# Modulation items of 1024 columns instead of 512 in a transformer kernel on one core

## The chip, the cores and the metric

The kernel runs on one core of a Trainium2 chip. The core has five engines with instruction queues of their own: TensorE (PE, with weight loads shown as PEld), VectorE (DVE), ScalarE (ACT), GpSimd (POOL) and SyncE (SP). Engines wait for each other by semaphores, and 16 DMA engines move data between HBM and the on-chip SBUF. The metric is the time of one execution in microseconds (us), measured on the device. All data are float32.

## The reference, cut to what matters

Eight sublayers work in turn on a sequence x of 256 tokens and 1024 features. In the first four (a hybrid mixer, a feed-forward layer, a dilated attention, a feed-forward layer) the normalized input is scaled and shifted, and the output gated, by vectors made from one conditioning vector c:

```python
def modulation(c, w, b):
    return jnp.split(jax.nn.silu(c) @ w + b, 3, axis=-1)

def sandwich(x, mod, g_pre, g_post, fn):
    shift, scale, gate = mod
    h = rms_norm(x, g_pre) * (1.0 + scale[:, None]) + shift[:, None]
    return x + gate[:, None] * rms_norm(fn(h), g_post)
...
        x = sandwich(x, modulation(c, ada_w[layer, 0], ada_b[layer, 0]), norm_pre[layer, 0], norm_post[layer, 0], mixer)
        x = sandwich(x, modulation(c, ada_w[layer, 1], ada_b[layer, 1]), norm_pre[layer, 1], norm_post[layer, 1], ffn)
```

So there are four modulations j = 0 to 3, each a vector of 1024 times a matrix `ada_w[j // 2, j % 2]` of 1024 rows and 3072 columns. Its columns are three parts of 1024: shift, scale and gate. Each matrix has 12 MB, and every element is used once.

## The kernel before

Every engine has one program, written out by hand; the order in the code is the order on the engine.

**Weights of the layers.** SP loads them in pieces of 1 MB into the six slots of `raw`. ScalarE casts a half of a piece (128 x 1024) to `whi` (L542), and VectorE subtracts it from the raw value to get the remainder `wlo` (L1299, called a split). TensorE multiplies with both. `whi` and `wlo` hold four halves. A raw slot is loaded again when VectorE has split both halves.

**Modulation.** The product of c with a matrix is not made on TensorE directly. VectorE multiplies 128 rows of a matrix with the matching 128 values of silu(c), which stand as a column `sc[:, k:k+1]`, and adds them to an accumulator (`acc_a` or `acc_b`, 128 partitions). After eight such items (k = 0 to 7) TensorE sums over the partitions with a matrix of ones (`sum_cols`, `sum_gates`). The first block of columns that TensorE needs (shift and scale of j = 0) comes through `raw` (`ada_first`) and isn't touched here. Everything later goes through `ada_ring`, which GpSimd fills: two halves, each of 4 row groups of 128 rows and 512 columns (1 MB). A half `kh` is loaded again when its four items are done:

```python
                        if b:
                            pool.wait_ge(s["ada_step"], 8 * (b - 1) + 4 * (kh + 1))
                        src, _ = src_cols(t["ada_w"][j // 2, j % 2], n, kh)
```

A block b has 512 columns and eight items, and there are 20 blocks (gate of j = 0, all of j = 1, 2, 3). VectorE works on them in `ada_item`, at places between its other work:

- In the hybrid mixer's input projection (`hyb_in`), two blocks and a half stand after groups of four splits. Then come the eight HGRN levels, `for i in range(8)`: `level(i)` (L1747 to L1749) multiplies decays, `merge(i - 1)` (L1731) picks scores, then a split, then one item (three at i = 6 and i = 7). TensorE's `level_scores(i)` waits for level and merge of the rounds before. L1719 is the product that opens the levels, L1764 the subtraction that gives the first half of `hlo` for the output projection.
- In the output projection, blocks 4 and 5; the last two items (k = 6, 7) of the last 512 scale columns are done by TensorE out of the ring (`PE_LAST`).
- In the first feed-forward layer, half a block at a time, after two splits.
- In the qkv projections, four splits (`proj`) and then a whole block of eight items, six times.

In the qkv stage TensorE needs four halves for a block of 512 output features: per half two groups of rows, four feature tiles and three products, 96 matmuls in all (`proj_half`, `three`).

Of the kernel before, what the change touches and what calls it, by code (L numbers as in the profile page):

```python
# [18 lines left out]
F32 = mybir.dt.float32  # L19
F32R = mybir.dt.float32r  # L20
ALU = mybir.AluOpType
# [67 lines left out]
def program(nc, t):  # L89

    with ExitStack() as ctx:
# [27 lines left out]
        with ExitStack() as first:  # L119
            ada_ring = sb(first, "ada_ring", [P, 2, 4, 512])  # L120
# [215 lines left out]
        DVE_LAST, PE_LAST = (4, 5), (6, 7)  # L336
# [117 lines left out]
        def _(pool):  # L454
            def ada_blocks(first, blocks):

                for i, (j, n) in enumerate(blocks):
                    b = first + i
                    for kh in range(2):
                        if b:  # L460
                            pool.wait_ge(s["ada_step"], 8 * (b - 1) + 4 * (kh + 1))
                        src, _ = src_cols(t["ada_w"][j // 2, j % 2], n, kh)
                        pool.dma_start(ada_ring[:, kh, :, :], src).then_inc(ada_in[kh], 16)  # L463
# [21 lines left out]
            SHIFT_SCALE, GATE = [0, 512, 1024, 1536], [2048, 2560]  # L485
            pool.wait_ge(s["ada_used"], ADA_FIRST)
            ada_blocks(0, [(0, n) for n in GATE])
            gain_row(0)
            ada_blocks(2, [(1, n) for n in SHIFT_SCALE])
            ada_blocks(6, [(1, GATE[0])])  # L490
            gain_row(1)
            ada_blocks(7, [(1, GATE[1])] + [(2, n) for n in SHIFT_SCALE + GATE])
# [5 lines left out]
            ada_blocks(14, [(3, SHIFT_SCALE[0])])  # L498
            gain_row(3)
            ada_blocks(15, [(3, n) for n in SHIFT_SCALE[1:] + GATE])  # L500
# [782 lines left out]
        def _(dve):  # L1283
# [18 lines left out]
            def ada_item(acc, b, n, k, it=0, bias=None):  # L1302

                kh, kk = k // 4, k % 4
                if kk == 0:
                    dve.wait_ge(ada_in[kh], 16 * (b + 1) + 32 * it)
                out = acc[:, bass.ds(n, 512)]
                if k == 0 and bias is not None:
                    dve.wait_ge(s[f"wrow_in{bias}"], 16)
                    ins = V.scalar_tensor_tensor(out=out, in0=ada_ring[:, kh, kk, :], scalar=sc[:, k:k + 1],  # L1310
                                                 in1=gg[:, bias, n:n + 512], op0=ALU.mult, op1=ALU.add)
                elif k == 0:
                    ins = V.tensor_scalar(out, ada_ring[:, kh, kk, :], sc[:, k:k + 1], None, ALU.mult)
                else:
                    dve.wait_ge(s["ada_step"], 8 * b + k + 16 * it)
# [4 lines left out]
            def ada_part(acc, b, n, kh, it=0, bias=None):  # L1320

                for kk in range(4):
                    ada_item(acc, b, n, 4 * kh + kk, it, bias)
# [1868 lines left out]
```

## Time and profile before

| what | value |
|---|---|
| median of 3 runs | 1269.61 us (1267.96 to 1271.66) |
| the profiled execution, its own time | 1269.97 us |
| its span, from the first to the last instruction | 1268.2 us |
| mean granted TensorE clock | 0.995 of full |
| TensorE busy | 1248.5 us (98%) |
| VectorE busy | 933.9 us (74%) |
| ScalarE busy | 718.2 us (57%) |
| moved by DMA | 274.41 MB, 216 GB/s over the span |

The profile is of one execution. Busy time is the time in which an engine has an instruction at work; the ends of matmuls are modelled, so a busy TensorE may hold short idle times. A share of the span is an average over stages whose limits differ.

### The profile page before, as it was taken

The numbers are of one execution on the slowest core, as the hardware profiler recorded it, in microseconds if no ns is written. First come the engines' busy times: TensorE is split into PE (matmuls) and PEld (weight loads), VectorE is DVE, ScalarE is ACT, GpSimd is POOL, SyncE is SP. The second block draws the span as 40 slices with busy tenths as digits, with TensorE's granted clock in tenths as the row PEclk, the third lists the DMA queues.
The fourth block names the chain that finished last, engine by engine and source line by source line (L and its number), as shares of the span: only waits on it lengthen the run. The fifth ranks groups of instructions, "written<-read, shape, count | busy, mean of one in ns | idle before, by whom it ended". The sixth has DMA issues, their size and how long they took to land.

```text
span 1268.2 us, 20841 instructions
## 1 busy us (share of the span) xinstructions
PE 1248.5 (98%) x8024; PEld 1133.6 (89%) x8024; DVE 933.9 (74%) x1222; ACT 718.2 (57%) x1069; POOL 50.8 (4%) x76
## 2 busy tenths in 40 slices
PE   8999999999999999999999999999999999999999
PEld 6998899999999778999989989888888888888888
DVE  6889988886899658666676695676666677666665
ACT  3676754444744557444467764665555667655554
POOL 1101000000111000000001000000000000000000
PEclk8999999999999999999999999999999999999999
DMA  9986989996799734666556544356565542366650
GB/s 348 372 297 208 339 290 325 334 327 205 244 361 370 230 67 153 206 203 200 199 166 211 162 150 155 132 198 200 200 202 202 190 163 95 122 220 204 202 166 34
DMA packets 147248, 274.41 MB, mean 216 GB/s; under 512 B 4759, under 2 KB 85679, under 8 KB 147048
## 3 DMA queue, kind: packets, MB, share of 16 engines
q1 hardware_dynamic: 132320, 220.21, 51.5%
q0 software_dynamic: 13616, 50.94, 11.9%
q10 hardware_dynamic: 1240, 2.26, 0.5%
q8 instruction: 49, 0.80, 0.3%
q14 instruction: 23, 0.19, 0.0%
HBM read 272.30 MB, written 1.10 MB: 216 GB/s over the span
## 4 chain that ended last, share of the span: by engine, by line
PE 82%; DVE 8%; DMA 4%; ACT 3%; issue 2%; ACTq 0%; POOL 0%; DVEq 0%; POOLq 0%
PE ps L2229 80%; DMA ada_ring<-in_ada_w 4%; DVE wlo L1299 2%; DVE acc_a L1316 2%; ACT whi L542 1%; PE ps L2682 1%; DMA voh<-in_voh 1%; ACT xn L603 0%; PE ps L2416 0%; PE ps L2399 0%; DVE rs L1949 0%; ACT h L659 0%; DVE prob L1906 0%; ACT hboth L654 0%; PE ps L2976 0%
## 5 line engine op out<-in xcount | busy, mean ns | idle before, releaser
L1299 DVE TENSOR_TENSOR wlo<-raw,whi 128x1024 fp32r<-128x1024 f32 x400 | 483.5, 1222 | 222.8 <-ACT whi L542 222.0
L542 ACT CAST whi<-raw 128x1024 fp32r<-128x1024 f32 x400 | 416.6, 1048 | 404.0 <-PE ps L2229 389.6
L2229 PE MATMUL ps<-hboth,whi 128*128 128x256 f32 (+1 forms) x2720 | 605.2, 311 | 1.0 <-DVE hboth L1529 0.5
L2229 PE MATMUL ps<-hboth,wlo 128*128 128x256 f32 x1792 | 491.6, 274 | 0.7 <-DVE hboth L1524 0.4
L2229 PEld LDWEIGHTS ps<-hboth,whi 128*128 128x128 f32 x2720 | 447.2, 191 | 30.1 <-issue 6.2
L2229 PEld LDWEIGHTS ps<-hboth,wlo 128*128 128x128 f32 x1792 | 343.9, 192 | 3.1 <-issue 0.6
L2229 PE MATMUL ps<-whi,hidhi 128*128 128x512 f32 x434 | 164.5, 379 | 0.0
L2229 PE MATMUL ps<-wlo,hidhi 128*128 128x512 f32 x434 | 164.1, 378 | 0.0
L2229 PE MATMUL ps<-whi,hidlo 128*128 128x512 f32 x434 | 164.1, 378 | 0.0
L2229 PE MATMUL ps<-whi,hboth 128*128 128x512 f32 (+1 forms) x512 | 155.8, 375 | 3.0 <-DVE wlo L1299 0.9
L2229 PEld LDWEIGHTS ps<-whi,hboth 128*128 128x128 f32 x512 | 95.5, 190 | 18.5 <-issue 5.1
L1316 DVE SCALAR_TENSOR_TENSOR acc_a<-ada_ring,sc,acc_a 128x512 f32<-128x512 f32 (+1 forms) x124 | 93.1, 751 | 7.6 <-DMA ada_ring<-in_ada_w 3.7
L2229 PE MATMUL ps<-wlo,hboth 128*128 128x512 f32 (+1 forms) x256 | 93.8, 366 | 0.0
L2229 PEld LDWEIGHTS ps<-whi,hidlo 128*128 128x128 f32 x434 | 82.0, 189 | 11.5
L2229 PEld LDWEIGHTS ps<-wlo,hidhi 128*128 128x128 f32 x434 | 82.1, 189 | 11.4 <-issue 0.2
L2229 PEld LDWEIGHTS ps<-whi,hidhi 128*128 128x128 f32 x434 | 82.2, 189 | 10.5 <-ACT whi L542 0.2
L2229 PEld LDWEIGHTS ps<-wlo,hboth 128*128 128x128 f32 x256 | 48.7, 190 | 6.2 <-issue 1.0
L463 POOL DMA_DIRECT2D ada_ring<-in_ada_w x40 | 30.0, 751 | 296.0 <-DVE acc_a L1316 212.6
L1651 DVE TENSOR_REDUCE tmp<-ps 128x512 f32<-128x1024 f32 x32 | 38.9, 1217 | 3.5 <-PE ps L2229 3.5
L1656 DVE TENSOR_TENSOR hidlo<-hid,hidhi 128x512 fp32r<-128x512 f32 x32 | 22.1, 692 | 16.6 <-ACT hidhi L760 16.6
L603 ACT ACTIVATE xn<-x 128x512 f32<-128x512 f32 (+1 forms) x32 | 19.3, 602 | 10.7 <-DVE x L1418 5.7
L755 ACT ACTIVATE tmp<-tmp 128x512 f32<-128x512 f32 x32 | 20.1, 627 | 2.9 <-DVE tmp L1651 2.9
(259 smaller groups left out, 1118.6 us busy)
## 6 DMA issues: line engine op xcount, KB each, us to landing
raw<-in_ffn_w_in SPq DMA_DIRECT2D x44, 1024.0 KB, 7.2
ada_ring<-in_ada_w POOLq DMA_DIRECT2D x40, 1024.0 KB, 7.9
raw<-in_w_mlp_up SPq DMA_DIRECT2D x32, 1024.0 KB, 5.4
raw<-in_w_mlp_down SPq DMA_DIRECT2D x32, 1024.0 KB, 4.9
raw<-in_ffn_w_out SPq DMA_DIRECT2D x22, 1024.0 KB, 5.1
raw<-in_att_w_qkv SPq DMA_DIRECT2D x18, 1024.0 KB, 7.3
raw<-in_w_in_even SPq DMA_DIRECT2D x18, 1024.0 KB, 5.1
raw<-in_hyb_w_in SPq DMA_DIRECT2D x10, 1024.0 KB, 11.2
```

The lines of the kernel that those rows point to most:

```text
L463: pool.dma_start(ada_ring[:, kh, :, :], src).then_inc(ada_in[kh], 16)
L542: A.copy(whi[:, H % 4, :], raw[:, slot(n), h * HALF:(h + 1) * HALF]).then_inc(s["hi_ready"], 1)
L603: A.activation(xn_of(j)[0][:, i // 2, c], x[:, i // 2, c], ACT.Square, accum_out=stat[:, 4 + i:5 + i]).then_inc(s["ssq_x"], 1)
L755: A.activation(tmp2[:, g % 3, :], tmp2[:, g % 3, :], ACT.Relu).then_inc(s["mrelu"], 1)
L1299: V.tensor_tensor(wlo[:, H % 4, :], raw[:, slot(n), h * HALF:(h + 1) * HALF], whi[:, H % 4, :].bitcast(F32), ALU.subtract).then_inc(s["lo_ ...
L1316: ins = V.scalar_tensor_tensor(out=out, in0=ada_ring[:, kh, kk, :], scalar=sc[:, k:k + 1], in1=out, op0=ALU.mult, op1=ALU.add)
L1651: V.tensor_reduce(in_order(tmp2[:, g % 3, :], 2), parts_of(UP_BANK[g % 3]), AX, ALU.add) \
L1656: V.tensor_tensor(hidlo2[:, g % 3, :], hid2[:, g % 3, :], hidhi2[:, g % 3, :].bitcast(F32), ALU.subtract).then_inc(s["mhid_lo"], 1)
L2229: return pe.matmul(out, lhsT, rhs, start=first, stop=last, skip_group_check=True)
L2682: m = pe.transpose(dl_turned(p, i)[:, (j - j0) * P:(j - j0 + 1) * P], dl_block(p, j), ident[:, :])
```

## The change

The blocks of 512 columns become whole parts of 1024 columns, w = 0 to 9. A load takes 256 rows (2 groups of 128) of a whole part instead of 512 rows of half a part. It still has 1 MB, but rows of 4 KB. The ring keeps its size: two slots of 1 MB, now `[P, 2, 2, D]`, and a slot is loaded again after two items. There are as many loads, 40, and half as many items. Where VectorE did eight items of a block it now does four items of 1024 columns. In the qkv stage they stand one by one between the splits. TensorE's share is now one item (k = 7) of all 1024 scale columns instead of two of 512.

```diff
-            ada_ring = sb(first, "ada_ring", [P, 2, 4, 512])
+            ada_ring = sb(first, "ada_ring", [P, 2, 2, D])
...
-        DVE_LAST, PE_LAST = (4, 5), (6, 7)
+        PE_LAST = 7
...
+            def ada_loads(first, rows):
+
+                for i, (j, n, q) in enumerate(rows):
+                    l = first + i
+                    if l >= 2:
+                        pool.wait_ge(s["ada_step"], 2 * (l - 1))
+                    src, _ = src_down(t["ada_w"][j // 2, j % 2][:, n:n + D], 2 * P * q)
+                    pool.dma_start(ada_ring[:, l % 2, :, :], src).then_inc(ada_in[l % 2], 16)
...
+            def ada_item(acc, w, n, k, it=0, bias=None):
+
+                q, kk = k // 2, k % 2
                 if kk == 0:
-                    dve.wait_ge(ada_in[kh], 16 * (b + 1) + 32 * it)
-                out = acc[:, bass.ds(n, 512)]
+                    dve.wait_ge(ada_in[q % 2], 16 * (2 * w + q // 2 + 1) + 32 * it)
+                out, row = acc[:, bass.ds(n, D)], ada_ring[:, q % 2, kk, :]
...
                     if ada:
-                        ada_part(*ada, 0, it, bias)
+                        ada_items(*ada, (4 * (g % 2), 4 * (g % 2) + 1), it, bias)
                     split_some(g, it, after[:2])
                     if ada:
-                        ada_part(*ada, 1, it)
+                        ada_items(*ada, (4 * (g % 2) + 2, 4 * (g % 2) + 3), it)
                     split_some(g, it, after[2:])
...
             proj("hyb_in", HYB[0:1], 0)
-            ada_block(acc_a, 0, 0, 0)
+            ada_items(acc_a, 0, 0, range(4), 0, 0)
             proj("hyb_in", HYB[1:2], 1)
-            ada_block(acc_a, 1, 512, 0)
+            ada_items(acc_a, 0, 0, range(4, 8))
             for q in range(4):
                 split(2 * (FIRST["hyb_in"] + 4) + 4 + q)
                 if q == 1:
-                    ada_part(acc_a, 2, 512 * 2, 0)
+                    ada_items(acc_a, 1, D, range(2))
...
-                for q in range(i, i + 1) if i < 6 else range(3 * i - 12, 3 * i - 9):
-                    b, k = (q + 20) // 8, (q + 20) % 8
-                    ada_item(acc_a, b, 512 * b, k)
-                    if q == 9:
-                        dve.wait_ge(s["hyb_hi"], 1)
-                        V.tensor_tensor(hlo[:, 0:4, :], y1[:, 0:4, :], hhi[:, 0:4, :].bitcast(F32), ALU.subtract) \
-                            .then_inc(s["hyb_lo"], 1)
-            ada_part(acc_a, 4, 512 * 4, 0)
+                if 1 <= i <= 6:
+                    ada_item(acc_a, 1, D, i + 1)
+                if i == 7:
+                    dve.wait_ge(s["hyb_hi"], 1)
+                    V.tensor_tensor(hlo[:, 0:4, :], y1[:, 0:4, :], hhi[:, 0:4, :].bitcast(F32), ALU.subtract) \
+                        .then_inc(s["hyb_lo"], 1)
+                    ada_item(acc_a, 2, 2 * D, 0)
+            ada_item(acc_a, 2, 2 * D, 1)
             split(2 * FIRST["hyb_in"] + 23)
-            ada_part(acc_a, 4, 512 * 4, 1)
+            ada_items(acc_a, 2, 2 * D, range(2, 4))
...
             for b in range(8):
-                proj("qkv", (QKV_B * 2 + QKV_A)[b:b + 1], b)
-                if b < 6:
-                    ada_block(acc_a, 14 + b, 512 * b)
+                for q in range(4):
+                    split(2 * (FIRST["qkv"] + 2 * b) + 4 + q)
+                    if b < 6:
+                        ada_item(acc_a, 7 + b // 2, D * (b // 2), 4 * (b % 2) + q)
...
             for i in range(16):
                 m = mm(ps[:, 0, i:i + P], acc_a[:, 1024 + i * P:1024 + (i + 1) * P], ones[:, :])
-                for k in PE_LAST if i >= 12 else ():
-                    m = mm(ps[:, 0, i:i + P], ada_ring[:, 1, k - 4, (i - 12) * P:(i - 11) * P],
-                           sc[:, k:k + 1].to_broadcast([P, P]), False, True)
-            m.then_inc(s["ada_step"], len(PE_LAST))
+                if i >= 8:
+                    m = mm(ps[:, 0, i:i + P], ada_ring[:, 1, 1, (i - 8) * P:(i - 7) * P],
+                           sc[:, PE_LAST:PE_LAST + 1].to_broadcast([P, P]), False, True)
+            m.then_inc(s["ada_step"], 1)
```

The instructions of VectorE in order, first where the last two HGRN levels stand. `acc_a` items are the modulation's, `wlo` is a split, `att` a merge, and `hboth<-y,hboth` the first `hlo` subtraction. Before:

```order
L1316 SCALAR_TENSOR_TENSOR acc_a<-ada_ring,sc,acc_a 128x512 [waits ada_step]
L1747 TENSOR_TENSOR bandqk<-pooled,tot 128x16x32 [waits hg_step,hg_copied,hg_scores]
L1748 TENSOR_TENSOR bandqk<-sq,tot 128x16x32
L1749 TENSOR_TENSOR f<-tot 128x16
L1299 TENSOR_TENSOR wlo<-raw,whi 128x1024 [waits hi_ready]
L1316 SCALAR_TENSOR_TENSOR acc_a<-ada_ring,sc,acc_a 128x512 [waits ada_step] x2
L1316 SCALAR_TENSOR_TENSOR acc_a<-ada_ring,sc,acc_a 128x512 [waits ada_step,ada_in1]
L1747 TENSOR_TENSOR pooled<-bandqk,f 128x8x64 [waits hg_step,hg_copied,hg_scores]
L1748 TENSOR_TENSOR sq<-bandqk,f 128x8x64
L1749 TENSOR_TENSOR tot<-f 128x8
L1316 SCALAR_TENSOR_TENSOR acc_a<-ada_ring,sc,acc_a 128x512 [waits ada_step]
L1764 TENSOR_TENSOR hboth<-y,hboth 128x1024 [waits hyb_hi]
```

and now (all lines of the kernel's VectorE part have moved by 1 or 5):

```order
L1321 SCALAR_TENSOR_TENSOR acc_a<-ada_ring,sc,acc_a 128x1024 [waits ada_step,ada_in1]
L1748 TENSOR_TENSOR bandqk<-pooled,tot 128x16x32 [waits hg_step,hg_copied,hg_scores]
L1749 TENSOR_TENSOR bandqk<-sq,tot 128x16x32
L1750 TENSOR_TENSOR f<-tot 128x16
L1304 TENSOR_TENSOR wlo<-raw,whi 128x1024 [waits hi_ready]
L1321 SCALAR_TENSOR_TENSOR acc_a<-ada_ring,sc,acc_a 128x1024 [waits ada_step]
L1748 TENSOR_TENSOR pooled<-bandqk,f 128x8x64 [waits hg_step,hg_copied,hg_scores]
L1749 TENSOR_TENSOR sq<-bandqk,f 128x8x64
L1750 TENSOR_TENSOR tot<-f 128x8
L1764 TENSOR_TENSOR hboth<-y,hboth 128x1024 [waits hyb_hi]
L1318 TENSOR_SCALAR acc_a<-ada_ring,sc 128x1024 [waits ada_in0]
L1321 SCALAR_TENSOR_TENSOR acc_a<-ada_ring,sc,acc_a 128x1024 [waits ada_step]
```

In level 6's round and after it, three items and one of 512 columns stood before level 7 and the `hlo` subtraction; now it is one of 1024, and the next part's first item follows the subtraction.

The second place is VectorE in the qkv stage, the sixth block of splits and items. Before:

```order
L1299 TENSOR_TENSOR wlo<-raw,whi 128x1024 [waits hi_ready] x4
L1313 TENSOR_SCALAR acc_a<-ada_ring,sc 128x512 [waits ada_in0]
L1316 SCALAR_TENSOR_TENSOR acc_a<-ada_ring,sc,acc_a 128x512 [waits ada_step] x3
L1316 SCALAR_TENSOR_TENSOR acc_a<-ada_ring,sc,acc_a 128x512 [waits ada_step,ada_in1]
L1316 SCALAR_TENSOR_TENSOR acc_a<-ada_ring,sc,acc_a 128x512 [waits ada_step] x3
```

and now:

```order
L1304 TENSOR_TENSOR wlo<-raw,whi 128x1024 [waits hi_ready]
L1321 SCALAR_TENSOR_TENSOR acc_a<-ada_ring,sc,acc_a 128x1024 [waits ada_step,ada_in0]
L1304 TENSOR_TENSOR wlo<-raw,whi 128x1024 [waits hi_ready]
L1321 SCALAR_TENSOR_TENSOR acc_a<-ada_ring,sc,acc_a 128x1024 [waits ada_step]
L1304 TENSOR_TENSOR wlo<-raw,whi 128x1024 [waits hi_ready]
L1321 SCALAR_TENSOR_TENSOR acc_a<-ada_ring,sc,acc_a 128x1024 [waits ada_step,ada_in1]
L1304 TENSOR_TENSOR wlo<-raw,whi 128x1024 [waits hi_ready]
L1321 SCALAR_TENSOR_TENSOR acc_a<-ada_ring,sc,acc_a 128x1024 [waits ada_step]
```

The four splits in a row and the eight items after them have become four pairs of a split and an item, and the waits for the two halves of the ring (`ada_in0`, `ada_in1`) now stand two splits apart. A tensor_scalar, which opens a part of columns, stands in every block before and in every second one now.

## Rows read from the trace of the kernel before

**Rows 1.** The page: busy time by engine, and the last chain's shares by engine.

```profile
PE 1248.5 (98%) x8024; PEld 1133.6 (89%) x8024; DVE 933.9 (74%) x1222; ACT 718.2 (57%) x1069; POOL 50.8 (4%) x76
...
PE 82%; DVE 8%; DMA 4%; ACT 3%; issue 2%; ACTq 0%; POOL 0%; DVEq 0%; POOLq 0%
```

**Rows 2.** Windows: us; busy us of PE, PEld, DVE, ACT, POOL; PEclk, DMA share, GB/s.

```profile
79.00:93.00 14.00, 13.15 (x82) 11.47 (x81) 14.00 (x17) 7.99 (x14) 0.75 (x1) 1.00 0.69 237
...
113.00:130.00 17.00, 15.65 (x83) 13.33 (x84) 14.99 (x21) 10.79 (x15) 2.25 (x3) 1.00 0.83 269
...
366.00:377.00 11.00, 11.00 (x101) 11.00 (x100) 10.02 (x13) 5.39 (x6) 1.50 (x2) 1.00 1.03 379
```

**Rows 3.** Timeline of VectorE, 36 to 135 us: start us, us, instruction, [idle before].

```profile
76.29 0.49 DVE L1313 TENSOR_SCALAR acc_a<-ada_ring,sc 128x512 f32<-128x512 f32 x1 [1.54 <-DMA ada_ring<-in_ada_w]
...
81.33 1.22 DVE L1719 TENSOR_TENSOR bandqk<-f 128x1024 f32<-128x1024 f32 x1
...
98.22 0.75 DVE L1316 SCALAR_TENSOR_TENSOR acc_a<-ada_ring,sc,acc_a 128x512 f32<-128x512 f32 x1
98.89 0.69 DVE L1747 TENSOR_TENSOR bandqk<-pooled,tot 128x512 f32<-128x512 f32 x1
...
109.81 2.38 DVE L1316 SCALAR_TENSOR_TENSOR acc_a<-ada_ring,sc,acc_a 128x512 f32<-128x512 f32 x3
112.11 0.69 DVE L1747 TENSOR_TENSOR pooled<-bandqk,f 128x512 f32<-128x512 f32 x1
...
114.05 1.22 DVE L1764 TENSOR_TENSOR hboth<-y,hboth 128x1024 fp32r<-128x1024 f32 x1
...
117.24 0.75 DVE L1313 TENSOR_SCALAR acc_a<-ada_ring,sc 128x512 f32<-128x512 f32 x1 [0.52 <-DMA ada_ring<-in_ada_w]
```

**Rows 4.** Timeline of TensorE at four of the level scores.

```profile
87.91 2.05 PE L2229 MATMUL ps<-pooled,sq 128*128 128x128 f32 x16 [0.60 <-DVE att L1731]
...
97.37 1.95 PE L2229 MATMUL ps<-pooled,sq 128*128 128x128 f32 x16
...
101.84 1.95 PE L2229 MATMUL ps<-bandqk 128*128 128x128 f32 x16
...
113.57 1.13 PE L2229 MATMUL ps<-pooled,sq 128*128 128x128 f32 x8 [0.85 <-issue]
```

**Rows 5.** Timeline of TensorE in the qkv stage, two of its repeating pieces.

```profile
365.07 0.39 PE L2229 MATMUL ps<-hboth,whi 128*128 128x256 f32 x2
...
365.41 0.39 PE L2229 MATMUL ps<-hboth,whi 128*128 128x256 f32 x2
```

**Rows 6.** Timeline of VectorE, qkv stage.

```profile
374.47 3.11 DVE L1316 SCALAR_TENSOR_TENSOR acc_a<-ada_ring,sc,acc_a 128x512 f32<-128x512 f32 x4 [0.56 <-DMA ada_ring<-in_ada_w]
377.50 4.62 DVE L1299 TENSOR_TENSOR wlo<-raw,whi 128x1024 fp32r<-128x1024 f32 x4
...
411.03 4.62 DVE L1299 TENSOR_TENSOR wlo<-raw,whi 128x1024 fp32r<-128x1024 f32 x4
```

**Rows 7.** Waits, 330 to 440 us: total us, times, longest us.

```profile
PE ps L2229 <- DVE wlo L1299: 0.9, 1, 0.9
```

**Rows 8.** Groups by line and shape, 0 to 430 us: count, busy us, mean ns.

```profile
L1316 DVE SCALAR_TENSOR_TENSOR acc_a<-ada_ring,sc,acc_a 128x512 f32<-128x512 f32 x82 | 61.6, 751 | 6.4 <-DMA ada_ring<-in_ada_w 3.7
...
L1455 DVE TENSOR_SCALAR xn<-x,small 128x1024 f32<-128x1024 f32 x2 | 1.5, 745 | 0.0
```

**Rows 9.** The tile ada_ring: count, ns min/median/max; and its transfers.

```profile
L1313 DVE TENSOR_SCALAR acc_a<-ada_ring,sc x16: 477/480/748, 76.3 to 404.3; 128x512 f32<-128x512 f32 x10, 128x512 f32 x6
...
DMA to landing us min/median/max: 5.6/7.9/10.8
```

**Rows 10.** The page's DMA issues: count, KB each, median us to landing.

```profile
raw<-in_w_mlp_up SPq DMA_DIRECT2D x32, 1024.0 KB, 5.4
raw<-in_w_mlp_down SPq DMA_DIRECT2D x32, 1024.0 KB, 4.9
```

**Rows 11.** Timeline of GpSimd: one issue of an ada load.

```profile
117.01 0.75 POOL L463 DMA_DIRECT2D ada_ring<-in_ada_w  x1 [4.63 <-DVE acc_a L1316]
```

More of the change, by code:

```diff
@@ L484, in _, with part_rows @@
             bias_row(1)
-            SHIFT_SCALE, GATE = [0, 512, 1024, 1536], [2048, 2560]
+            def part_rows(j, part):
+                return [(j, part * D, q) for q in range(4)]
+            SHIFT, SCALE, GATE = range(3)
             pool.wait_ge(s["ada_used"], ADA_FIRST)
-            ada_blocks(0, [(0, n) for n in GATE])
+            ada_loads(0, part_rows(0, GATE))
             gain_row(0)
-            ada_blocks(2, [(1, n) for n in SHIFT_SCALE])
-            ada_blocks(6, [(1, GATE[0])])
+            ada_loads(4, part_rows(1, SHIFT) + part_rows(1, SCALE))
+            ada_loads(12, part_rows(1, GATE)[:2])
             gain_row(1)
-            ada_blocks(7, [(1, GATE[1])] + [(2, n) for n in SHIFT_SCALE + GATE])
+            ada_loads(14, part_rows(1, GATE)[2:])
+            ada_loads(16, part_rows(2, SHIFT) + part_rows(2, SCALE) + part_rows(2, GATE))
             gain_row(2)
@@ L1300, in split, with ada_items @@
                                 whi[:, H % 4, :].bitcast(F32), ALU.subtract).then_inc(s["lo_ready"], 1)
[L1302 to L1304 removed]
+            def ada_item(acc, w, n, k, it=0, bias=None):
+                q, kk = k // 2, k % 2
                 if kk == 0:
[L1306 to L1307 removed]
+                    dve.wait_ge(ada_in[q % 2], 16 * (2 * w + q // 2 + 1) + 32 * it)
+                out, row = acc[:, bass.ds(n, D)], ada_ring[:, q % 2, kk, :]
                 if k == 0 and bias is not None:
                     dve.wait_ge(s[f"wrow_in{bias}"], 16)
[L1310 to L1311 removed]
+                    ins = V.scalar_tensor_tensor(out=out, in0=row, scalar=sc[:, k:k + 1], in1=gg[:, bias, :],
+                                                 op0=ALU.mult, op1=ALU.add)
                 elif k == 0:
[L1313 removed]
+                    ins = V.tensor_scalar(out, row, sc[:, k:k + 1], None, ALU.mult)
                 else:
[L1315 to L1317 removed]
+                    dve.wait_ge(s["ada_step"], 8 * w + k + 8 * it)
+                    ins = V.scalar_tensor_tensor(out=out, in0=row, scalar=sc[:, k:k + 1], in1=out, op0=ALU.mult,
+                                                 op1=ALU.add)
                 ins.then_inc(s["ada_step"], 1)
[L1320 to L1323 removed]
+            def ada_items(acc, w, n, ks, it=0, bias=None):
+                for k in ks:
+                    ada_item(acc, w, n, k, it, bias)
             def ada_first(a):
```

39 lines of the change are left out of this document (13 added, 26 removed).

## Prediction

> **What bounds the kernel now.** I read the page first. TensorE is busy for 98% of the span, VectorE for 74%, and the chain that ended last is 82% TensorE, 8% VectorE and 4% DMA [rows 1]. Freed VectorE time is therefore worth something only where TensorE stands still for VectorE. The second view is the table of stretches: see where TensorE's busy time falls short of the window. It does so in 79 to 93 us (13.15 of 14.00, VectorE busy 14.00 of 14.00) and in 113 to 130 us (15.65 of 17.00); in 366 to 377 us it is not short at all (11.00 of 11.00), while the DMA share is 1.03 [rows 2]. So two places matter: the HGRN levels inside the first projection, where VectorE is the packed engine, and the qkv projections, where the transfers are.
>
> In the levels, see two waits of TensorE: before the scores at 87.91 us it stood 0.60 us for VectorE's merge (L1731), and before those at 113.57 us 0.85 us [rows 4]; the latter follow level 7 of VectorE, which starts at 112.11 us because three items of modulation stand before it from 109.81 us [rows 3]. In the qkv stage the whole loss is one wait of 0.9 us for a split [rows 7], that of the burst at 411.03 us [rows 6].
>
> How much is there to win? The shortfalls of the two windows are 0.85 + 1.35 us, with the 0.9 us of the qkv stage 3.1 us. The ends of matmuls are modelled, so some idle time may be hidden; I allow up to 4.5 us. All other stretches with modulation run with TensorE full or wait for something else.
>
> **The change, part by part.**
>
> *The items.* 160 items of 512 columns (158 on VectorE, 2 on TensorE) become 80 of 1024 (79 and 1). A scalar_tensor_tensor of 512 takes 751 ns [rows 8]. No trace row has one of 1024 with both inputs in SBUF, so I take the slope of tensor_tensor: 0.69 us for 512 columns (98.89 us) and 1.22 us for 1024 (114.05 us) [rows 3], so 0.53 us for 512 more columns, and 1.28 us for the item. The bounds are 1.22 us (the tensor_tensor itself) and 1.50 us (twice the small one, nothing saved). A tensor_scalar goes from 480 ns [rows 9] to 745 ns [rows 8]. Before there are 142 x 0.751 + 16 x 0.49 = 114.5 us; after, 71 x 1.28 + 8 x 0.745 = 96.9 us: some 17.6 us less VectorE work of 933.9 [rows 1]. Nearly all of it lies under TensorE work or before a DMA landing, and is worth nothing. The cover is TensorE's own matmuls, and it is thin only at the two places.
>
> *Head of the levels.* The tensor_scalar at 76.29 us starts when its load lands (1.54 us idle for the DMA) [rows 3]. It and the three items behind it last 0.49 + 3 x 0.78 = 2.8 us; the new pair lasts 0.745 + 1.28 + 0.03 = 2.06 us, so 0.75 us less. The load was asked for after the items of the loads before it, which are shorter by some 0.5 us a load, but it may then wait behind other transfers; I take 0.25 us earlier, between 0 and the 1.0 us that two such loads make. L1719 then moves from 81.33 to about 80.3 us (79.6 to 80.6).
>
> *The levels.* From L1719 to the first hlo subtraction at 114.05 us there are now ten small items. From start to start an item between others costs 0.67 us (98.22 to 98.89), three in a row 2.30 us (109.81 to 112.11) [rows 3], the tensor_scalar 0.48 - 0.08 = 0.40 us. In all 4 x 0.67 + 0.40 + 0.67 + 2.30 + 0.66 = 6.7 us. In their place come six large ones at 1.28 - 0.08 = 1.20 us, 7.2 us. So the chain grows by 0.5 us, and it also changes shape. The item before level 1 is gone, which removes the 0.60 us wait at 87.91. Levels 2 to 6 each get 1.20 - 0.67 = 0.53 us more. TensorE's pace there is 4.47 us a level (scores at 97.37 and 101.84 us [rows 4]); VectorE, which just keeps it now, needs 5.0 us. The lead is eaten up, and the scores of the last levels come at the old time or 0.1 us later. At level 7 one item stands in the way instead of three. The hlo subtraction starts at 114.05 - 1.0 + 0.5 = 113.55 us, and the output projection that waits for it 0.5 us earlier. TensorE then has work without a gap up to the next norm, so 0.5 us is what remains. Bounds: -1.2 us (L1719 at 79.6 us); at 1.50 us an item, seven of them 0.22 us dearer, -0.5 + 1.5 = +1.0 us, with a late landing +1.2 us.
>
> *The qkv stage.* TensorE needs 3 matmuls in 0.34 us (365.07 to 365.41) [rows 5] and a block has 96, 10.7 us. VectorE's blocks come every (411.03 - 377.50) / 3 = 11.18 us [rows 6]. This builds up the delay that ends in the 0.9 us. A block needs two raw and two ada loads of 1.05 MB; at 379 GB/s [rows 2] four take 11.1 us. So DMA sets the pace already, and lighter items cannot change that. What the change moves is the request. A half of the ring is now asked for again after item, split, item (1.20 + 1.15 + 1.28 = 3.6 us) instead of four items (3.1 us at 374.47 us [rows 6]). With the median landing of 7.9 us [rows 9] and the 0.2 us that 11.18 - 3.1 - 7.9 leaves for the hand-over, the ring's round is 11.7 us instead of 11.2 us. I take 11.1 us, because that landing time is itself queueing behind the raw loads, and spaced requests queue less. Rows of 4 KB instead of 2 KB may help: loads of 1024 KB land after 5.4 us with rows of 1 KB and after 4.9 us with rows of 4 KB [rows 10]. Half of it, 0.25 us a load, I count as 0.4 us less of the last wait. Bounds: -0.9 us (the wait is gone), +2.6 us (five rounds at 0.52 us more, if the landing time stays at 7.9 us).
>
> *The rest.* The split of the last scale columns on TensorE stays at eight products. In the feed-forward stage two items of 2.5 us replace four of 3.0 us under TensorE work that has no gap; without the cover they would save, not cost. The two loads that precede the qkv stage are asked for where they were.
>
> **Sum.** -0.5 (levels) - 0.4 (qkv) = -0.9 us on the profiled execution's 1269.97 us: 1269.1 us. The median of the runs shown is 0.36 us under that execution, so I forecast **1268.7 us**. A measurement of this kernel can tell about 0.3%, 3.8 us, from no change; my bounds add up to -2.1 and +3.8 us.
>
> **A rule weighed.** A tensor_scalar of 512 columns takes 480 ns as a rule, but 748 ns at most [rows 9]: the one at 117.24 us took 0.75 us, while GpSimd was issuing a load from 117.01 to 117.76 us [rows 3, 11]. The two got into each other's way. [...] By the row, five rounds with two such meetings are 1.5 us, and with the other terms the time is 1270.2 us.
>
> **The rivals.**
> 1. *Both stalls vanish.* For it: VectorE's head start of 1 us, three items fewer before level 7, 4 KB rows. Against it: ten small items become six large ones at the very engine that is full. Price: all of the 3.1 to 4.5 us, so 1265.1 to 1266.5 us. Chance 0.20, of which 0.12 beyond 3.8 us.
> 2. *The ring's round governs qkv (slower).* Place: VectorE's wait for ada_ring between two splits. For it: VectorE already waits there (0.56 us at 374.47 [rows 6]), and the request now comes 0.5 us later in the round. Against it: the DMA queue, not the round, is full. Price: (3.6 + 0.2 + L) - 11.18 us a block over five blocks. At L = 7.9 us it gives +2.6 and, with nothing won in the levels, 1272.2 us; from L = 8.15 us on it passes 3.8 us: 1273.5 us and more. Chance 0.15, of which 0.10 beyond 3.8 us.
> 3. *The item of 1024 saves little.* At 1.50 us each the levels lose 1.0 us instead of winning 0.5, and the qkv stage loses its 0.4 us: 1270.6 us. Chance 0.05, of which 0.01 beyond. The ports' collision of the row at 117.24 us, 1270.2 us as worked out above: chance 0.05, of which 0.01 beyond.
> 4. *It does nothing that shows,* VectorE's saved time turns into idle time: that is the forecast, and with 1267.3 to 1270.5 us it has 0.55.
>
> **The numbers.** Faster by over 0.3%: 0.12 from rival 1 and 0.02 for something unseen, 0.14. Slower: 0.10 + 0.02 + 0.02, 0.14. Within: 0.72. For 8 in 10 I take 1265.2 (rival 1) to 1272.7 us (rival 2 at L = 7.9 us and a little more).
>
> **What would show it right or wrong.** VectorE's busy time near 916 us. The item of 1024 at 1.28 us. L1719's successor at about 80.3 us, the wait before level 2's scores gone, that before the last scores still there. DVE waits for ada_ring in the qkv stage of some 1.5 to 2 us a block, about 10 us in all, as the burst of splits no longer covers the landing, while TensorE's wait at the end of the stage is 0 to 1 us. I am wrong if TensorE waits for splits in several qkv blocks, if landing takes over 8.5 us, or if the levels' scores run at 5 us from level 3 on.

## The result

The changed kernel takes 1274.27 us (median of 10 runs, 1272.85 to 1281.04), the kernel before 1269.89 us (10 runs beside it). The ratio is 1.0037, with a 95% interval of 1.0026 to 1.0048: slower by 4.4 us. The forecast was 1268.7 us, 1265.2 to 1272.7. It was wrong: the time lies above the range. To a kernel slower by over 3.8 us I had given 0.14.

The page of the changed kernel answers to [rows 1]. VectorE has lost 17.4 us where 17.6 us were forecast, and TensorE's work is as it was:

```profile
PE 1249.3 (98%) x8024; PEld 1135.9 (89%) x8024; DVE 916.5 (72%) x1143; ACT 719.0 (57%) x1069; POOL 48.9 (4%) x76
...
L1321 DVE SCALAR_TENSOR_TENSOR acc_a<-ada_ring,sc,acc_a 128x1024 f32<-128x1024 f32 (+1 forms) x62 | 79.8, 1288 | 16.3 <-DMA ada_ring<-in_ada_w 15.4
```

The last figures of the second row are the reading: VectorE's items stood idle 15.4 us for the ring's loads. So the time went where VectorE waits for transfers. The stretches of the changed kernel, beside [rows 2], say which place that is. Columns are us, busy us of PE, PEld, DVE, ACT and POOL, then PEclk, DMA share and GB/s:

```profile
79.00:93.00 14.00, 14.00 (x94) 13.06 (x94) 13.76 (x15) 9.89 (x14) 0.00 (x0) 1.00 0.70 242
93.00:113.00 20.00, 19.08 (x167) 18.50 (x165) 19.97 (x27) 11.72 (x20) 2.10 (x3) 1.00 0.62 211
113.00:130.00 17.00, 16.25 (x85) 13.81 (x86) 12.63 (x14) 12.53 (x18) 1.41 (x2) 1.00 0.91 304
355.00:411.00 56.00, 51.42 (x429) 49.95 (x428) 41.61 (x36) 24.02 (x25) 7.13 (x10) 1.00 0.97 342
```

The second and the last of these stretches in the kernel before:

```profile
93.00:113.00 20.00, 19.72 (x176) 19.53 (x175) 19.86 (x29) 13.04 (x22) 1.50 (x2) 1.00 0.47 164
355.00:411.00 56.00, 55.89 (x457) 54.49 (x456) 51.87 (x61) 26.59 (x26) 8.23 (x11) 1.00 1.02 370
```

In the levels TensorE is fuller than before in two stretches (14.00 of 14.00 us against 13.15, 16.25 of 17.00 against 15.65) and emptier in the one between them (19.08 of 20.00 against 19.72), 0.81 us fuller in all. In the qkv stage it has become 4.5 us emptier, and the DMA engines have become emptier too: 342 GB/s where they had moved 370. Both engines that I had taken for the possible bounds of that stage have idle time in it. What is busy is the hand-over between them, as VectorE's timeline in the changed kernel shows (start us, us, instruction, [idle before]):

```profile
368.94 0.75 DVE L1318 TENSOR_SCALAR acc_a<-ada_ring,sc 128x1024 f32<-128x1024 f32 x1 [1.83 <-DMA ada_ring<-in_ada_w]
369.60 1.22 DVE L1304 TENSOR_TENSOR wlo<-raw,whi 128x1024 fp32r<-128x1024 f32 x1
370.74 1.28 DVE L1321 SCALAR_TENSOR_TENSOR acc_a<-ada_ring,sc,acc_a 128x1024 f32<-128x1024 f32 x1
371.93 1.22 DVE L1304 TENSOR_TENSOR wlo<-raw,whi 128x1024 fp32r<-128x1024 f32 x1
374.84 1.28 DVE L1321 SCALAR_TENSOR_TENSOR acc_a<-ada_ring,sc,acc_a 128x1024 f32<-128x1024 f32 x1 [1.69 <-DMA ada_ring<-in_ada_w]
376.04 1.22 DVE L1304 TENSOR_TENSOR wlo<-raw,whi 128x1024 fp32r<-128x1024 f32 x1
...
387.12 1.28 DVE L1321 SCALAR_TENSOR_TENSOR acc_a<-ada_ring,sc,acc_a 128x1024 f32<-128x1024 f32 x1 [2.23 <-DMA ada_ring<-in_ada_w]
```

and GpSimd's, which asks for the loads:

```profile
378.76 0.70 POOL L462 DMA_DIRECT2D ada_ring<-in_ada_w  x1 [5.74 <-DVE acc_a L1321]
```

Follow one half of the ring once round. Its first item starts at 374.84 us. The split at 376.04 and the second item follow, and at 378.76, 3.9 us after the start, the half is asked for again. Its next first item starts at 387.12 us, when the load has landed, 8.4 us later: a round of 12.3 us, and VectorE stood 2.23 us for it. The split that TensorE needs next stands behind that item. Blocks start at 352.91 us (the second) and 414.66 us (the seventh), 12.35 us apart, where the prediction had read 11.18 us before. TensorE now waits for splits in three blocks instead of one by the profile's count (waits of 340 to 425 us: total us, times, longest us; before, [rows 7]):

```profile
DVE acc_a L1321 <- DMA ada_ring<-in_ada_w: 13.0, 7, 3.6
...
PE ps L2230 <- DVE wlo L1304: 3.7, 3, 2.1
```

A fourth wait, 0.84 us before TensorE's instruction at 377.36 us, is booked as "issue", but it ends just behind the split that ran from 376.04 to 377.26 us.

One split ahead of the stage and one behind it give its length. In the kernel before they start at 337.96 and 436.01 us, 98.05 us apart. In the changed kernel:

```profile
337.14 1.23 DVE L1304 TENSOR_TENSOR wlo<-raw,whi 128x1024 fp32r<-128x1024 f32 x1
...
439.90 1.23 DVE L1304 TENSOR_TENSOR wlo<-raw,whi 128x1024 fp32r<-128x1024 f32 x1 [0.99 <-ACT whi L547]
```

That is 102.76 us: the stage has lost 4.71 us. Ahead of it the kernel was 0.82 us early (337.14 against 337.96), and behind it nothing changes. 4.71 - 0.82 = 3.89 us, and the two spans differ by 3.9 us (1268.2 and 1272.1). So the loss lies in the stage. These are two single executions; what the 0.82 us are worth is said below.

### The profile page after: what moved, and what is told of

It reads as the page before. It is cut to its first block, busy times and chain, and to the rows that moved or that the text cites. A ratio compares the mean times of both kernels' runs of the same rounds, so it can differ in the third digit from the quotient of the medians.

```text
span 1272.1 us, 20743 instructions
## 1 busy us (share of the span) xinstructions
PE 1249.3 (98%) x8024; PEld 1135.9 (89%) x8024; DVE 916.5 (72%) x1143; ACT 719.0 (57%) x1069; POOL 48.9 (4%) x76
## 4 chain that ended last, share of the span: by engine, by line
PE 82%; DVE 7%; DMA 4%; ACT 3%; issue 3%; ACTq 0%; POOL 0%; DVEq 0%; POOLq 0%
PE ps L2230 81%; DMA ada_ring<-in_ada_w 3%; DVE wlo L1304 2%; DVE acc_a L1321 1%; ACT whi L547 1%; PE ps L2683 1%; DMA voh<-in_voh 1%; ACT xn L608 0%; PE ps L2417 0%; PE ps L2400 0%; DVE rs L1950 0%; ACT h L664 0%; DVE prob L1907 0%; ACT hboth L659 0%; PE ps L2977 0%
## 5 line engine op out<-in xcount | busy, mean ns | idle before, releaser
L2230 PEld LDWEIGHTS ps<-wlo,hidhi 128*128 128x128 f32 x434 | 82.3, 190 | 11.2 <-issue 0.2
L1321 DVE SCALAR_TENSOR_TENSOR acc_a<-ada_ring,sc,acc_a 128x1024 f32<-128x1024 f32 (+1 forms) x62 | 79.8, 1288 | 16.3 <-DMA ada_ring<-in_ada_w 15.4
```

The costliest lines, as they stand in the source:

```text
L1321: ins = V.scalar_tensor_tensor(out=out, in0=row, scalar=sc[:, k:k + 1], in1=out, op0=ALU.mult, op1=ALU.add)
L2230: return pe.matmul(out, lhsT, rhs, start=first, stop=last, skip_group_check=True)
```

## The experiments

Theory A is the round: hold of a half of the ring (from its first item's start to the request for its next load), then the landing. If the sum is above what TensorE needs for a block, the ring paces the stage. The rivals blame the new items, rows and loads themselves (B), or the rate of the DMA engines (C). "Stage" below is the distance of the two splits just used. In each experiment all else is the kernel named.

**The old order with the new items.** In the changed kernel:

```diff
                 for q in range(4):
                     split(2 * (FIRST["qkv"] + 2 * b) + 4 + q)
-                    if b < 6:
-                        ada_item(acc_a, 7 + b // 2, D * (b // 2), 4 * (b % 2) + q)
+                if b < 6:
+                    ada_items(acc_a, 7 + b // 2, D * (b // 2), range(4 * (b % 2), 4 * (b % 2) + 4))
```

> The changed kernel, with the qkv stage's VectorE order put back: four splits, then four items of 1024 columns. Theory A (a ring slot's round, from its first item of a block to the load that replaces it, sets the pace of the qkv stage, and the splits between the items lengthen it): the round is two items at 1.20 us from start to start, 0.2 us to the request and 8.0 to 8.5 us to the landing, 10.6 to 11.1 us, below TensorE's own 11.15 us a block, so TensorE does not wait; what is left of the change is the 0.7 to 0.8 us gained in the levels: 0.6 us below the kernel before, 5 us below the changed kernel, about 1269.2 us. Rival B (items of 1024 columns, rows of 4 KB or loads of 256 rows are themselves slow beside the rest): the qkv stage stays 4 us longer, about 1273 us or more, since all the work now comes in one piece. Rival C (the DMA engines have not the bandwidth for the stage): as B.

Measured: 1267.66 us (11 runs), ratio to before 0.998 [0.997, 0.999]. The stage takes 96.52 us. The direction is A's, and B and C fall: width, rows, loads and bytes are the changed kernel's, and only the places of the items moved back. The gain is larger than expected: 2.0 us below the kernel before instead of 0.6, because the stage is 1.53 us shorter than in the one profiled execution of the kernel before, where I had expected it equal. Against the changed kernel it is 6.24 us shorter: so much does the order alone cost there. The stretch of 355 to 411 us in this kernel has TensorE full and the DMA engines faster than either kernel had them:

```profile
355.00:411.00 56.00, 56.00 (x456) 54.63 (x455) 48.79 (x42) 26.66 (x27) 7.15 (x10) 1.00 1.02 376
```

**The new order with the old items.** In the kernel before:

```diff
             for b in range(8):
-                proj("qkv", (QKV_B * 2 + QKV_A)[b:b + 1], b)
-                if b < 6:
-                    ada_block(acc_a, 14 + b, 512 * b)
+                for q in range(4):
+                    split(2 * (FIRST["qkv"] + 2 * b) + 4 + q)
+                    if b < 6:
+                        ada_item(acc_a, 14 + b, 512 * b, 2 * q)
+                        ada_item(acc_a, 14 + b, 512 * b, 2 * q + 1)
```

> The kernel before, with one edit: in the qkv stage two items of 512 columns behind each split instead of eight behind four splits. Theory A: a slot is now held for four items at 0.78 us and a split at 1.14 us, 4.3 us instead of 3.1; with 0.2 and 8.0 to 8.5 us the round is 12.5 to 13.0 us against TensorE's 11.15, over five rounds 6.5 to 9 us, of which about 1.5 us is covered by the lead that TensorE's buffers give: 5 to 7.5 us above the kernel before, 1275 to 1277.5 us. Rival B (width, rows or loads of the new items): nothing of them is in this kernel, so 1269.9 us, as before. Rival C: no byte moves that did not move before, 1269.9 us.

Measured: 1277.47 us (6 runs), ratio 1.0062 [1.0047, 1.0077]; the stage takes 106.61 us, 8.56 us more than before. Blocks start 12.79 us apart (354.42 to 418.39 us for five). Nothing of the new items, rows or loads is in this kernel. The order alone makes it slower than either.

**Two splits inside a hold.** In the changed kernel the order item, split, split, item:

```diff
                 for q in range(4):
+                    if b < 6 and q % 2 == 0:
+                        ada_item(acc_a, 7 + b // 2, D * (b // 2), 4 * (b % 2) + q)
                     split(2 * (FIRST["qkv"] + 2 * b) + 4 + q)
-                    if b < 6:
+                    if b < 6 and q % 2:
                         ada_item(acc_a, 7 + b // 2, D * (b // 2), 4 * (b % 2) + q)
```

> The changed kernel, with the qkv stage's order item, split, split, item: two splits while a slot is held instead of one, the number of splits, items and bytes as it was. Theory A: each round grows by a split, 1.14 us, to 13.2 to 13.5 us; over five rounds 4 to 6 us above the changed kernel, 1278 to 1280 us. Rivals B and C: the same work, bytes and loads, 1274.3 us within 1 us.

Measured: 1278.66 us (6 runs), ratio 1.0072 [1.0058, 1.0087]. The time is where A put it, but that is luck, for the reason given was half wrong. Blocks start 12.44 us apart (358.72 to 408.48 us for four), not 13.2 or more, and the stage takes 104.62 us, 1.9 us more than in the changed kernel and not 4 to 6. The hold grew as expected, from 3.9 to 5.05 us up to the request (357.52 to 362.57 us), but the landing fell from 8.4 to 7.4 us (the loads of GpSimd in this stage):

```profile
DMA to landing us min/median/max: 6.7/7.4/8.5
```

The sum of the two, 5.05 + 7.4, is 12.45 us, so the form of the theory stands; that the landing is a constant does not. Some 2 us of this kernel's profiled time arise ahead of its first split (38.35 us against 36.24 in the changed kernel), where the kernels do the same. That split starts between 34.69 and 38.35 us in the eleven profiled executions, but here all six runs are at 1277.89 us or more; that part I did not explain.

**Four slots.** In the changed kernel, with its order, the ring's 2 MB in four slots of 128 rows (the waits of SyncE, TensorE and VectorE follow the slots; 80 loads of 512 KB; two more semaphores come in, an unused one goes and two later uses share one):

```diff
-            ada_ring = sb(first, "ada_ring", [P, 2, 2, D])
+            ada_ring = sb(first, "ada_ring", [P, 4, D])
...
-                    if l >= 2:
-                        pool.wait_ge(s["ada_step"], 2 * (l - 1))
-                    src, _ = src_down(t["ada_w"][j // 2, j % 2][:, n:n + D], 2 * P * q)
-                    pool.dma_start(ada_ring[:, l % 2, :, :], src).then_inc(ada_in[l % 2], 16)
+                    if l >= 4:
+                        pool.wait_ge(s["ada_step"], l - 3)
+                    src = t["ada_w"][j // 2, j % 2][P * k:P * (k + 1), n:n + D]
+                    pool.dma_start(ada_ring[:, l % 4, :], src).then_inc(ada_in[l % 4], 16)
```

> The changed kernel with its order, and the ring in the same 2 MB cut into four slots of 128 rows, each loaded and freed by one item (80 loads of 512 KB instead of 40 of 1 MB). Theory A: a slot is held for one item only, 1.3 us, and has the whole 11.15 us of a block to come back, so a landing of up to 9.6 us is hidden: no wait in the qkv stage, 0.7 us below the kernel before, about 1269.2 us. Rival C (bandwidth of the DMA engines): the same bytes in the same time, so it stays near 1274 us. Rival B (1024-column items or 4 KB rows): near 1274 us too. [...]

Measured: 1267.84 us (12 runs), ratio 0.9987 [0.9977, 0.9997]; the stage takes 96.52 us, to the hundredth that of the old order. Its stretch of 355 to 411 us and a piece of VectorE's timeline:

```profile
355.00:411.00 56.00, 56.00 (x456) 54.64 (x455) 48.57 (x42) 26.66 (x27) 10.02 (x18) 1.00 1.03 394
```

```profile
374.47 1.22 DVE L1304 TENSOR_TENSOR wlo<-raw,whi 128x1024 fp32r<-128x1024 f32 x1 [0.26 <-ACT whi L547]
375.62 1.28 DVE L1319 SCALAR_TENSOR_TENSOR acc_a<-ada_ring,sc,acc_a 128x1024 f32<-128x1024 f32 x1
377.16 1.23 DVE L1304 TENSOR_TENSOR wlo<-raw,whi 128x1024 fp32r<-128x1024 f32 x1 [0.27 <-ACT whi L547]
```

The order between the splits is harmless once a slot is held by one item and has a whole block to come back. The smaller loads also land sooner (median 6.6 us). VectorE now waits before its splits for ScalarE (which follows TensorE), and before its items for a load only once, 0.4 us. GpSimd's doubled requests (20 in the stage of 0.53 us each, against 10 of 0.70 us in the changed kernel) cost nothing that shows. And 394 GB/s were to be had, where the prediction called the queue full at 379. Its blocks start 10.72 us apart (371.80 to 393.24 us for two): that is TensorE's own pace, the 10.7 us of the prediction. The 11.15 and 11.06 us a block that some of the expectations give to TensorE are too long.

**Pairs.** In the changed kernel the order split, split, item, item:

```diff
                     split(2 * (FIRST["qkv"] + 2 * b) + 4 + q)
-                    if b < 6:
-                        ada_item(acc_a, 7 + b // 2, D * (b // 2), 4 * (b % 2) + q)
+                    if b < 6 and q % 2:
+                        ada_items(acc_a, 7 + b // 2, D * (b // 2), range(4 * (b % 2) + q - 1, 4 * (b % 2) + q + 1))
```

> The changed kernel, with the qkv stage's order split, split, item, item: the items still lie between splits, but no split lies between the two items of one slot. Theory A (the round of a slot counts, and only the split inside it lengthens it): a slot is held 2.4 us as in the order four and four, round 10.6 to 11.1 us, 1267.7 us within 0.7 us. Rival D (any item that waits for its load in front of a split holds up TensorE, wherever it stands): items stand in front of splits twice as often as in the order four and four, so about half of the changed kernel's loss comes back, 1270 to 1272 us.

Measured: 1267.47 us (11 runs), ratio 0.998 [0.9971, 0.9989]; stage 96.52 us. This is A's time, not D's. It isn't the items ahead of splits that cost, it is the split inside a hold. This is the fastest kernel of the study, though the old order and the four slots lie within 0.4 us of it.

**Narrow operations in the old order.** The kernel of the first experiment, with each qkv item as two operations (c is 0 and 512), and the step counted after the second:

```diff
-                    ada_items(acc_a, 7 + b // 2, D * (b // 2), range(4 * (b % 2), 4 * (b % 2) + 4))
+                    for k in range(4 * (b % 2), 4 * (b % 2) + 4):
+                        ada_two(7 + b // 2, D * (b // 2), k)
```

> The kernel of the order four and four, with each qkv item of 1024 columns worked off as two operations of 512 columns; loads, ring and everything before the qkv stage as there. Theory A: a slot is held 3.1 us instead of 2.4 us, as in the kernel before, and the round is back at 11.1 to 11.2 us, so the 1.1 us by which the order four and four came out below levels' 0.8 us is lost again: 1268.7 us within 0.5 us. Rival E (the gain beyond 0.8 us comes from the loads of 256 rows or from the levels alone): 1267.7 us, no change.

Measured: 1268.31 us (11 runs), ratio 0.999 [0.998, 0.9999]; stage 97.31 us. The time is in A's range, but its interval also covers that of the first experiment; the stage tells A from E. Of the 1.53 us by which the old order's stage is shorter than that of the kernel before, 0.79 us come back with the longer hold. The other 0.74 us I can't place: loads of 256 rows instead of 512, or other arrival times, are left.

**Both cures together.** The four slots in the order of four and four; the two diffs above.

> The four slots of 128 rows together with the order four splits, four items. Theory A: either edit alone has taken the ring's round below TensorE's 11.06 us a block, so the two together give no more than one: 1267.7 us within 0.5 us. Rival F (the DMA engines' rate still costs something in either of them, and the two add): 1266.5 us or less.

Measured: 1268.06 us (12 runs), ratio 0.9992 [0.9983, 1.0002]; stage 96.53 us. One cure is enough, TensorE is the floor, and rival F falls.

**Half the weights beside it.** In the changed kernel, SyncE's loads for the stage:

```diff
                 dst = raw[:, slot(n), :].rearrange("p (k n) -> p k n", k=k)
+                if FIRST["qkv"] <= n < FIRST["att_out"]:
+                    dst, ap = dst[:, 0:2, :], ap[:, 0:2, :]
```

> The changed kernel and its order, but the qkv stage's weight loads (the other user of the DMA engines there) bring only the first 256 of their 512 rows, 512 KB instead of 1 MB each; the second half of each raw tile keeps old data, and all operations of the engines run as before, so the output is not the reference's. Theory A says that the round is hold + 0.2 us + landing and that the landing of 8.4 us is made by the weight loads beside it: it should fall to 5.5 to 7 us, the round to under 11 us, and the 5 us of TensorE's waits in the stage disappear, 1267.5 to 1268.5 us. Rival G (the order itself, VectorE's items between the splits or the slower GpSimd request, costs the time whatever the landing): 1273 to 1274 us.

Measured: 1268.55 us (12 runs), ratio 0.999 [0.9981, 1.0000]; stage 96.53 us, with the changed kernel's order and engine work. The loads of both queues in the stage (count, KB, median us to landing), of this kernel:

```profile
ada_ring<-in_ada_w POOLq DMA_DIRECT2D x10, 1024.0 KB, 6.7
raw<-in_att_w_qkv SPq DMA_DIRECT2D x10, 512.0 KB, 4.5
```

The landing fell from 8.4 to 6.7 us, and with it all of the stage's loss. Rival G falls: without a long landing the order costs nothing. This run alone would fit rival C too, since it moves fewer bytes; C fell with the runs that move all of them.

**Four splits inside a hold.** In the changed kernel the order item, four splits, three items:

```diff
+                if b < 6:
+                    ada_item(acc_a, 7 + b // 2, D * (b // 2), 4 * (b % 2))
                 for q in range(4):
                     split(2 * (FIRST["qkv"] + 2 * b) + 4 + q)
-                    if b < 6:
-                        ada_item(acc_a, 7 + b // 2, D * (b // 2), 4 * (b % 2) + q)
+                if b < 6:
+                    ada_items(acc_a, 7 + b // 2, D * (b // 2), range(4 * (b % 2) + 1, 4 * (b % 2) + 4))
```

> The changed kernel with the qkv order item, split, split, split, split, item, item, item: the slot of the first two items is held for all four splits, 6.9 us, the other for 2.4 us. The order with two splits inside had made the stage 1.9 us longer than the changed kernel's, not the 5.7 us of five splits, with its landing down from 8.4 to 7.4 us. Theory A with a landing that stays between 7.4 and 8.4 us: round of the first slot 14.5 to 15.5 us, stage 10 to 15 us longer than the changed kernel's, 1284 to 1290 us. Rival H (the landing gives back what the hold takes, the round stays near 12.5 us): 1274 to 1277 us.

Measured: 1291.03 us (5 runs), ratio 1.0167 [1.0153, 1.0181], just above the range of A and far from H. VectorE's timeline of this kernel, and the landing of its ring loads in the stage:

```profile
371.93 0.75 DVE L1318 TENSOR_SCALAR acc_a<-ada_ring,sc 128x1024 f32<-128x1024 f32 x1 [5.67 <-DMA ada_ring<-in_ada_w]
372.59 4.62 DVE L1304 TENSOR_TENSOR wlo<-raw,whi 128x1024 fp32r<-128x1024 f32 x4
377.14 3.98 DVE L1321 SCALAR_TENSOR_TENSOR acc_a<-ada_ring,sc,acc_a 128x1024 f32<-128x1024 f32 x3
386.19 1.28 DVE L1321 SCALAR_TENSOR_TENSOR acc_a<-ada_ring,sc,acc_a 128x1024 f32<-128x1024 f32 x1 [5.07 <-DMA ada_ring<-in_ada_w]
```

```profile
DMA to landing us min/median/max: 7.1/7.5/8.1
```

The half is held from 371.93 us to the request at 378.71 us, and the next item starts at 386.19: 6.8 + 7.5 = 14.3 us. The landing does not shrink further, though the engines move only 284 GB/s here. The stage takes 119.20 us; its blocks come 14.7 us apart (356.53 to 415.48 us for four).

The rounds side by side, in us. Hold is from the first item's start to the request, for a half that does not open with the shorter tensor_scalar (such a hold is up to 0.5 us less); only the first row and the four splits are means over both. The landing is the stage's median for GpSimd's loads, and TensorE's floor is 10.72 us a block. Blocks are taken from the second to the seventh, or, where the text above names four, over those; the 11.2 us are the prediction's:

```
kernel                         hold   landing   sum    blocks apart   stage
kernel before                   3.3     7.8     11.1      11.2        98.05
changed kernel                  3.9     8.4     12.3      12.35      102.76
old items, new order            4.4     8.6     13.0      12.8       106.61
two splits inside               5.05    7.4     12.45     12.4       104.62
four splits inside              7.1     7.5     14.6      14.7       119.20
new items, old order            2.9     8.0     10.9      10.9        96.52
pairs                           2.9     8.2     11.1      10.9        96.52
narrow operations, old order    3.2     7.9     11.1      11.1        97.31
half the weights                3.9     6.7     10.6      10.8        96.53
```

Where VectorE waits for every load, a round is hold plus landing by its very meaning, so the match of the third and fourth columns proves little. What the experiments show is that the stage grows and shrinks with these two, whatever the items, their order and the bytes are. The sums are no sharp test near the floor. With 10.9 and 11.1 us the old order and the pairs are 0.2 and 0.4 us above TensorE's 10.72 us and TensorE still does not wait for a split; my estimate is that VectorE's lead covers the 1 to 2 us that five such rounds make.

## Why the prediction was wrong, step by step

*The items: right.* 1.28 us was forecast for an item of 1024 columns and 1.28 us is measured in the qkv stage (up to 1.35 us inside the levels); VectorE's busy time of about 916 us is 916.5. An item of 1024 columns is 15% cheaper than two small ones (1.50 us); that is real, and worth next to nothing outside the levels, as the prediction said: TensorE is the full engine.

*Head of the levels and the levels: the places came as forecast, the gain is not shown.* L1719's successor was to move from 81.33 to 80.3 us and starts at 79.88. The wait of 0.60 us before level 2's scores is gone (14.00 of 14.00 us busy in 79 to 93), that before the last scores stayed (0.73 us), and the stretch that was to win 0.5 us won 0.82 us in this pair of executions. The rows that show it, the head of the levels and the first hlo subtraction in the changed kernel:

```profile
75.61 0.75 DVE L1318 TENSOR_SCALAR acc_a<-ada_ring,sc 128x1024 f32<-128x1024 f32 x1 [0.66 <-DMA ada_ring<-in_ada_w]
...
79.88 1.22 DVE L1720 TENSOR_TENSOR bandqk<-f 128x1024 f32<-128x1024 f32 x1
...
113.44 1.23 DVE L1764 TENSOR_TENSOR hboth<-y,hboth 128x1024 fp32r<-128x1024 f32 x1 [0.47 <-ACT hboth L878]
```

But the kernel with the old items in the new order is the kernel before up to the qkv stage, and in its profiled execution the 0.60 us wait is gone too:

```profile
79.00:93.00 14.00, 14.00 (x93) 12.82 (x92) 14.00 (x16) 9.58 (x14) 0.75 (x1) 1.00 0.74 254
```

From the program's first split to the split ahead of the stage it takes 300.18 us (37.20 to 337.38 us), the kernel before 301.92 us, the changed kernel 300.90 us, and the eight others with the new items 300.40 to 301.01 us. Two executions of the same instructions differ by more than the gain. The medians leave some 0.3 to 0.9 us for it when the stage's difference is taken off (four slots 1.8 - 1.5, pairs 2.4 - 1.5), which lies inside their intervals. So the levels are not where the forecast failed, but no run shows that they won anything.

*The qkv stage: this step failed.* It had the right sum on paper: item, split, item, 3.6 + 0.2 + 7.9 = 11.7 us, against 11.2 us before. Then it set the sum aside with two statements, and with them it priced VectorE's longer wait for the ring at nothing. The first was "So DMA sets the pace already". It rested on a DMA share of 1.03 at 379 GB/s [rows 2] and on four loads filling 11.1 of 11.18 us. The four slots, the old order and the pairs show it false for the changed kernel: with the same bytes the DMA engines moved 394, 376 and 382 GB/s in 355 to 411 us, at a share of 1.02 to 1.03, and the blocks came 10.7 to 10.9 us apart. That the 11.18 us of before were already the ring's round, 3.3 + 7.8, fits the table but is argued: no run shortened the round of the old loads of 2 KB rows. The second was "I take 11.1 us, because that landing time is itself queueing behind the raw loads, and spaced requests queue less". The landing is indeed made longer by the raw loads (8.4 us, and 6.7 us when they are halved), but spacing the requests did not shorten it: 8.4 us against 8.0 with the new loads, 8.6 against 7.8 with the old. In the experiment with two splits inside the hold it was shorter again, 7.4 us. I suppose that it depends on where the request falls among the raw loads; that was not tested, and I cannot say in advance which way it goes. The term was taken at -0.4 us with a bound of +2.6; it measured +4.7 us. The mis-sized term is the landing: it was taken from the whole trace (7.9 us), and 0.5 us more in each of five rounds are 2.5 us.

*Rival 2 is what happened.* Its place (VectorE's wait between two splits) and its mechanism are those of the trace, and it named 1273.5 us and more from a landing of 8.15 us; at the 8.4 us measured the same sum, (3.6 + 0.2 + 8.4) - 11.18 five times over, is 5.1 us, and 1274.7 us. What I held against it, "the DMA queue, not the round, is full", is the same false statement. A chance of 0.15 was too low for a rival whose sum came from rows, against a forecast whose value came from an argument.

*What would show it wrong.* The first sign came: TensorE waits for splits in three blocks (3.7 us). The second did not, the landing's median is 8.4 us and not over 8.5. The third came in part: the scores of levels 5 and 6 stand 4.8 and 4.9 us behind those before them, against 4.47 us in the kernel before, and the last scores were not late by it. VectorE waits for the ring 15.4 us in the stage (13.0 us of its longer items, 2.4 us of the tensor_scalars), not about 10.

*A tensor_scalar beside a request* was not put to a test by the change. In the changed kernel all eight tensor_scalar operations take 748 to 754 ns, and none is lengthened. In the qkv stage none runs beside a request of GpSimd: they start at 345.3, 368.94 and 392.41 us, the requests before them at 366.27 and 391.04 us and 0.70 us long. So no run shows the 1.5 us that the prediction set down for two such meetings, nor a collision at ports: in the changed kernel there was no meeting and no longer operation. The row that the prediction showed does come again: with the old items in the new order the tensor_scalar at 116.61 us takes 0.76 us beside a request from 116.39 to 117.14 us, against 0.48 us as a rule. But in the same kernel one at 408.35 us takes 0.49 us, though its first 0.21 us lie beside a request for `dbias` that ends at 408.56 us. Why two were longer and one was not, no run shows. The gain of 4 KB rows, of which the prediction made 0.25 us a load, did not appear as a shorter landing (7.8 us before, 8.4 us after, 8.0 us in the old order).

## What to carry to other kernels

Where a ring of buffers feeds an engine, add up its round: the time that a buffer is held, the request, the landing under the load of that very stage. Compare that with what the bounding engine needs for the same work. When the sum is the longer of the two, all that is put between the first and the last use of a buffer is paid for in every round; put it between two buffers instead, or cut the same memory into more slots, each freed by one operation. A DMA share near 1 does not prove that the bytes are the limit. A run with the round shortened tells: at 1.02 the stage had moved 370 GB/s, and at 1.03 it moved 394. The same stretch of two executions of one program can differ by more than the gain that one looks for (here 1.7 us ahead of the stage); read it in more than one trace.

## What the runs showed of the hardware

The landing of GpSimd's 1 MB loads depends on what shares the DMA engines: 8.4 us in the changed kernel, 6.7 us with the weights halved. It does not follow the mean rate: it was 7.5 us with four splits inside the hold, where the engines moved 284 GB/s, and 8.0 us in the old order, where they moved 376. How long such a load takes alone, none of these stretches shows.

The longest stalls of TensorE, 3.1 us in one kernel and 3.5 to 3.9 us in another, were followed by a slower clock. In the kernel with old items in the new order TensorE stood for 3.1 us of the stretch 390 to 394 us; its granted clock was 1.00 before, and 0.53 on the mean of the next 6 us of full work (us, busy us of PE, PEclk, DMA share, GB/s):

```profile
383.00:390.00 7.00, 7.00 (x65) 1.00 1.01 351
390.00:394.00 4.00, 0.90 (x9) 0.84 0.78 297
394.00:400.00 6.00, 6.00 (x30) 0.53 0.87 315
400.00:410.00 10.00, 10.00 (x92) 1.00 1.01 370
```

The changed kernel's waits of up to 2.1 us drew no such fall (PEclk 1.00 in its stretch of 355 to 411 us). The kernel with four splits inside has such a dip as well, 0.66 in 389 to 394 us, behind a stall of 3.9 us. In the kernel with old items 30 recorded matmuls fill the 6 us that at full clock hold about 55 (92 in 10 us), so by this estimate the dip cost 2.7 us beside the stall of 3.1 us. That such dips are why these two kernels came out at the top of what was expected of them, or above it, was not tested.
